# A two-layer diffusion trunk with mixture of experts: the barrier behind the expert loops taken out, layer 1's first adaLN units moved up to them, and the q and k weights issued earlier

## The reference, cut to what matters

```python
for l in range(DEPTH):                       # DEPTH = 2
    mod = split(silu(c) @ ada_w[l] + ada_b[l], 6)          # adaLN shifts, scales, gains
    h = modulate(rmsnorm(x, g[0]), mod[0], mod[1])
    y = mixer(h, ...)                                      # mLSTM, pooling, attention
    x = x + mod[2] * rmsnorm(y, g[1])
    h2 = modulate(rmsnorm(x, g[2]), mod[3], mod[4])
    x = x + mod[5] * rmsnorm(ec_moe(h2, ...), g[3])        # 16 experts, each picks its tokens
    # layer 0 does the same for the context stream
```

## Time and profile before

| | us |
|---|---|
| median of three runs | 2609.04 |
| the three runs | 2605.70, 2609.04, 2611.33 |
| span of the profiled execution | 2604.5 |
| PE busy in it | 2364.8 (91%) |
| DVE, ACT, POOL busy | 694.2, 649.7, 572.9 |

### The profile page before, as it was taken

The page is one execution under the profiler, slowest core; times in us unless marked ns, Lnnn a source line. Parts: engine busy times, 40 slices in busy tenths (PEclk is TensorE's granted clock), DMA queues, the critical chain, the costliest instruction groups (busy, mean ns, idle before and its releaser), DMA issues.

```text
span 2604.5 us, 38764 instructions
## 1 busy us (share of the span) xinstructions
PE 2364.8 (91%) x16132; PEld 1541.6 (59%) x16132; DVE 694.2 (27%) x1403; ACT 649.7 (25%) x1144; POOL 572.9 (22%) x314
## 2 busy tenths in 40 slices
PE   4999999999987699999997699999999689988986
PEld 3778878888876344444443577877887533333332
DVE  3261073101022311111101625054112332222223
ACT  4263253222123110111111435343223301110001
POOL 1143321343510011111111324333465000000000
PEclk8999999999999899999998799999999889999998
DMA  6271440222224699999999336333233579999996
GB/s 241 94 265 64 126 117 14 80 66 86 69 97 160 251 388 390 390 389 392 391 389 354 130 125 248 85 101 86 94 128 110 208 313 402 411 412 410 413 413 251
DMA packets 179894, 596.06 MB, mean 229 GB/s; under 512 B 16040, under 2 KB 57392, under 8 KB 167152
## 3 DMA queue, kind: packets, MB, share of 16 engines
q1 hardware_dynamic: 166448, 563.29, 57.4%
q0 software_dynamic: 10304, 25.99, 3.6%
q10 hardware_dynamic: 3040, 5.31, 0.6%
HBM read 576.63 MB, written 21.07 MB: 229 GB/s over the span
## 4 chain that ended last, share of the span: by engine, by line
PE 69%; DMA 21%; DVE 3%; issue 3%; ACT 2%; POOL 1%; POOLq 0%; SPq 0%; DVEq 0%; ACTq 0%
PE ps L443 19%; PE ps L938 15%; DMA ring_lo<-in_w_gate 11%; PE ps L438 10%; PE ps L858 6%; PE ps L948 6%; DMA zone<-in_w_up 5%; PE ps L879 4%; DMA ring_lo<-in_ada_w 3%; PE ps L754 1%; PE ps L771 1%; PE ps L452 1%; PE ps L957 1%; DMA ring_lo<-in_w_in 1%; PE ps L740 1%
## 5 line engine op out<-in xcount | busy, mean ns | idle before, releaser
L443 PE MATMUL ps<-hi_r,ring_r 128*128 128x512 f32 (+1 forms) x1792 | 474.7, 353 | 3.2 <-POOL ring_r L1870 3.2
L938 PE MATMUL ps<-ring_lo,zone 128*32 128x256 f32 (+1 forms) x3072 | 438.2, 492 | 31.0 <-DMA ring_lo<-in_w_gate 26.8
L443 PEld LDWEIGHTS ps<-hi_r,ring_r 128*128 128x128 f32 x1792 | 316.5, 190 | 50.6 <-POOL ring_r L1870 3.7
L938 PEld LDWEIGHTS ps<-ring_lo,zone 128*32 128x32 f32 (+1 forms) x3072 | 156.5, 124 | 306.4 <-issue 278.9
L1870 POOL TENSOR_TENSOR ring_r<-ring_lo,ring_r 128x2048 fp32r<-128x2048 f32 (+1 forms) x58 | 241.9, 4176 | 367.4 <-ACT ring_r L1031 333.9
L443 PE MATMUL ps<-lo_r,ring_r 128*128 128x512 f32 (+1 forms) x896 | 315.3, 352 | 0.0
L948 PE MATMUL ps<-zone 128*64 128x512 f32 (+1 forms) x2048 | 289.2, 493 | 0.8
L438 PE MATMUL ps<-ring_r,hi_r 128*128 128x512 f32 x736 | 233.2, 398 | 7.1 <-POOL ring_r L1870 6.6
L1981 POOL DMA_INDIRECT zone<-xn_dram,zone x36 | 40.4, 1122 | 843.4 <-DVE zone L1843 769.8
L948 PEld LDWEIGHTS ps<-zone 128*64 128x64 f32 (+1 forms) x2048 | 110.4, 124 | 162.8 <-issue 142.4
L443 PEld LDWEIGHTS ps<-lo_r,ring_r 128*128 128x128 f32 x896 | 169.8, 189 | 23.2
(11 more groups left out here) (303 smaller groups left out, 2771.1 us busy)
## 6 DMA issues: line engine op xcount, KB each, us to landing
ring_lo<-in_w_gate SPq DMA_DIRECT2D x64, 2048.0 KB
zone<-in_w_down SPq DMA_DIRECT2D x64, 2048.0 KB, 22.5
ring_lo<-in_w_up SPq DMA_DIRECT2D x32, 2048.0 KB
zone<-in_w_up SPq DMA_DIRECT2D x32, 2048.0 KB
ring_lo<-in_w_in SPq DMA_DIRECT2D x52, 1024.0 KB
ring_lo<-in_ada_w SPq DMA_DIRECT2D x24, 2048.0 KB
ring_lo<-in_w_branch SPq DMA_DIRECT2D x24, 512.0 KB, 6.2
zone<-v_dram SPq DMA_DIRECT2D x128, 64.0 KB, 1.9
```

Source lines behind the costliest of these rows:

```text
L443: i = mm(dst[:, t0:t0 + tw], b[:, kk, f * P:(f + 1) * P], a[:, k, t0:t0 + tw], start=start and n == 0, stop=stop and n == 2)
L938: i = mm(bank(((2, 4), (3, 5))[s // 2][gi])[j * M:(j + 1) * M, 0:W], xeT[:, k, c0:c0 + M], w[:, k % 4, j * W:(j + 1) * W], start=(k == 0), ...
```

## The change

Five things change.

1. The last `phase_end` of both layers (`ph + 4`) goes on all four engines, and `NPH` becomes 3.
2. adaLN unit 3 goes to slot 3 (in `zone`) in place of slot 0, and SP issues it right behind units 0 to 2.
3. SP issues `("qk", 0)`, the three small loads and `("qk", 1)` of layer 1 ahead of the six loads of `moe_dram`. `("qk", 0)` has slot 1 and waits until PE has used adaLN unit 1; `("qk", 1)` has slot 2 and waits for unit 2.
4. In layer 1 ACT makes the high parts of q and k, ahead of its first square; POOL no longer does.
5. POOL subtracts for the first half at once, and for the second half when five tiles of `x` are there.

```diff
-        ORDER = ((("ada", 0), 0), (("ada", 1), 1), (("ada", 2), 2), (("ada", 3), 0), ...
+        ORDER = ((("ada", 0), 0), (("ada", 1), 1), (("ada", 2), 2), (("ada", 3), 3), ...
...
-        NPH = 4
+        NPH = 3
...
-                phase_end(pe, ph + 4)
...
                 else:
+                    for half in range(2):
+                        _, slot, count, _, _ = units[l, "qk", half]
+                        act.wait_ge(w_ready(slot), 16 * count)
+                        A_(unit_hi(slot, ring_r), unit_lo(slot), ACT.Copy).then_inc(sem("q_hi"), 1)
                     for t in range(NT + 1):
...
-                phase_end(act, ph + 4)
...
-                phase_end(dve, ph + 4)
...
-                if h < 2:
+                if h < 2 and l == 0:
                     pool.wait_ge(w_ready(slot), 16 * units[(l,) + SPLITS[h]][2])
                     G.tensor_copy(unit_hi(slot, ring_r), unit_lo(slot)).then_inc(sem("p_hi"), 1)
-                    pool.wait_ge(sem("p_hi"), 2 * l + h + 1)
+                    pool.wait_ge(sem("p_hi"), h + 1)
+                elif h < 2:
+                    pool.wait_ge(sem("q_hi"), h + 1)
...
+                split(l, 0)
                 if not first:
                     pool.wait_ge(sem("x_tile"), NT - 1)
-                split(l, 0)
...
-                phase_end(pool, ph + 4)
...
-                    return k_[0] > 0 and k_[1] == "ada" and k_[3] < 4
+                    return k_[0] > 0 and (k_[1] == "qk" or k_[1] == "ada" and k_[3] < 4)
...
                 if l + 1 < DEPTH:
-                    for j in range(3):
+                    for j in range(4):
                         load((l + 1, "ada", l + 1, j))
+                    load((l + 1, "qk", 0))
+                    load_vectors(l + 1)
+                    load((l + 1, "qk", 1))
                 if l == 0:
                     sp.wait_ge(sem("y_added"), 16 * len(SETS[l]) * NE)
                     for t in range(nt(l)):
                         sp.dma_start(xn[:, t, :], moe_dram[l][t * P:(t + 1) * P, :]).then_inc(sem(f"moe_in{t}"), 16)
                 if l + 1 < DEPTH:
-                    load((l + 1, "ada", l + 1, 3))
                     sp.wait_ge(sem("x_tile"), l * PER["x_tile"] + NT)
```

More of the change, by code:

```diff
@@ L302, in kn512 @@
             return w[:, c:c + 512].rearrange("(k p) n -> p k n", p=P)
-        ORDER = ((("ada", 0), 0), (("ada", 1), 1), (("ada", 2), 2), (("ada", 3), 0), (("qk", 0), 1), (("qk", 1), 2), (("v", 0), 0),
+        ORDER = ((("ada", 0), 0), (("ada", 1), 1), (("ada", 2), 2), (("ada", 3), 3), (("qk", 0), 1), (("qk", 1), 2), (("v", 0), 0),
                  (("v", 1), 1), (("ada", 4), 2), (("ada", 5), 0), (("ada", 6), 1), (("ada", 7), 2), (("ada", 8), 0), (("o", 0), 1),
@@ L2050, in load_branch, with load_vectors @@
                     sp.dma_start(branch_w(q, False).rearrange("p (k n) -> p k n", k=KB), src).then_inc(sem(f"mg_in{q % 2}"), 16)
-                def load_vectors():
+                def load_vectors(l):
                     sp.wait_ge(sem("pads_set"), 1)
@@ L2072, in _ @@
                     if key[1:] == ("qk", 0):
-                        load_vectors()
+                        load_vectors(l)
                     if key[1:] == ("vn", 0):
```

## The result

The changed kernel takes 2612.05 us, median of 20 runs (2606.79 to 2615.54); the kernel before 2607.86, median of 20 (2604.49 to 2611.33). The ratio is 1.0016, 95% interval 1.001 to 1.0022: slower by 4.2 us. The forecast was 2.5 less than before, 2606.5, with a range of 2601 to 2612; the sign is wrong, and the time is just outside the range.

What follows compares the result with a forecast made beforehand. PE, busy 91% of the span, was taken as the bound, so only its idle time at two places could move: +0.4 at the layer boundary and −2.9 at layer 1's end gave −2.5 us, 2606.5, range 2601 to 2612.

Steps and rivals of the forecast that it cites:

- The barrier after layer 0: Between layers 0 and 1: without it ACT could begin 1.1 us earlier, and PE's adaLN units move up to 1412.1.
- The loads put ahead of the sums: At the layer boundary: the experts' sums are issued 4.4 us later, and ACT's first square begins 6.4 later, at 1433.0.
- the rival of the late sums: At the boundary: ACT begins at 1437.7, 4.7 us more, so the whole is +2.2, 2611.2, no change; chance 0.12.
- what it called wrong: Sign at the boundary: prediction wrong if ACT's first square is before 1430 or after 1438, or no DVE instruction is stretched.
- The wait of ACT for unit 3 goes: In layer 1's chain of tiles: ACT no longer waits for adaLN unit 3 before `ada_rows`, a gain of 5.0 us.
- POOL's second subtraction: Behind the fifth tile of x: it holds DVE's last tile for 4.6 us, bounds 0 and 5.1.
- the rule on two SBUF inputs: At DVE's L1403 and L1405: two-SBUF-input instructions and GpSimd instructions reading SBUF exclude each other, costing 4.6 us.
- POOL's wait goes: At layer 1's first q and k product: POOL's first subtraction ends before 1435, PE no longer waits, gain 5.6 us.
- The barrier at the end of layer 1: At the end of layer 1: ACT starts beside DVE's additions, so the last stretch starts 2.9 us earlier, bounds 0 and 3.0.

Runs made afterwards that it cites:

- e1: The changed kernel with one lone drain of POOL behind layer 0's expert loop, on which no engine waits: 2606.99 us, ratio 0.9995 to the kernel before.
- e4: The kernel before with only the last barriers of both layers taken out: 2605.81 us, ratio 0.9998.
- e7: The changed kernel with a drain of POOL in every turn of layer 0's expert loop: 2608.06 us, ratio 1.0006 to the kernel before.
- e2: The changed kernel with the three small loads issued behind the experts' sums: 2607.47 us, ratio 1.0002 to the kernel before.
- e5: The changed kernel with the edits of e1, e2 and e3 together: 2600.83 us, ratio 0.9976 to the kernel before.
- e6: The changed kernel with e1's drain, sums issued before q, k and small loads, ACT's copies behind `ada_rows`, both POOL subtractions behind the sixth tile: 2601.15 us, ratio 0.9981.
- e3: The changed kernel with POOL's second subtraction waiting for the sixth tile of x, not the fifth: 2607.34 us, ratio 1.0002 to the kernel before.
- e8: The kernel before with only the barrier at the end of layer 1 taken out: 2602.85 us, ratio 0.9989.

## Why the prediction was wrong, by its own steps

*"The barrier after layer 0": this step failed.* It priced the barrier by who waits at that place, 1.1 us for ACT, and took the 4.06 of the drain to vanish with it. e1, e4 and e7 show that the work of a drain is kept and done by POOL's next one. There the kernel waits for it. That the drain cost little where it stood is right: without the barrier e4's first square comes 1.0 earlier. What the prediction didn't ask is what comes due later on POOL if the drain is gone. In the changed kernel that is 4.0 (5.80 for 1.78, and PE's wait 9.79 for 5.78); the stretch has 4.4, and e1 gives back 4.5, both with its scatter. The term stood at nothing in the sum, and in every rival.

*"The loads put ahead of the sums": the mechanism right, the size 5.0 short; this term failed too.* The prediction had the first square 6.4 later, from a down product that ends at 1412.1; against that end it came 11.4 later (25.95 less 14.56). Of the 5.0, 0.9 is the issue of `("qk", 0)`, at +5.0 for +4.1, since PE used unit 1 later; 3.3 is SP, which took 13.3 from there to `("qk", 1)`, not the 10.0 of the earlier trace rows, nor the 11.3 of the earlier trace rows; 0.9 is the landing of the second half, 5.9 for 5.0.

It is the rival of the late sums, which had 0.12: 20.9 and its 4.7 make +25.6, and +25.95 is 0.3 past it. The profile's own 1436.9 looks to be inside the bounds (1431.7 to 1437.7) only because this execution ended its down product 1.1 earlier; on the prediction's scale it is 1438.0, at the very edge of what it called wrong.

The 10.0 had been read as the price of three small issues. The traces fit another reading, which no run tests by itself: it is the time until the load ahead of them has landed. In the kernel before, `("qk", 0)` landed at 1464.7 and SP came free of the small loads at 1464.2; in the changed one that load took 13.5 us to land,

```profile
DMA to landing us min/median/max: 13.5/13.5/13.5
```

that is until 1429.4, and SP came free at 1429.2. In e2, e5 and e6 too SP is free of the three 0.2 to 0.4 before the last big load ahead has landed. And the queue itself ran late: by PE's matmuls unit 2 was there at +9.7 and unit 3 at +15.6 (+6.9 and +12.3 forecast). What held the queue up is not shown.

*"The wait of ACT for unit 3 goes": right.* PE has used unit 3 by 1428.5, and no wait of ACT before `ada_rows` is left.

*"POOL's second subtraction": right, 4.2 for 4.6.* The held instruction is L1432 (4.91 less 0.75), a TENSOR_SCALAR that reads SBUF, for which the prediction had no row; e3 moves the hold behind the last tile and PE starts 3.8 earlier. The forecast leaned on the wrong rule for it. It named the rule on two SBUF inputs and looked for the hold at L1403 and L1405; the hold came on the TENSOR_SCALAR ahead of them, and whether the subtraction would have held those two no row here shows. The Trainium skill ("SBUF — State Buffer", section "Who interferes with whom") has a second rule that bears on it: copies and TENSOR_SCALAR can run in a mode that uses both port pairs, and then they exclude GpSimd too. This case's rows agree: TENSOR_SCALAR 4.91 for 0.75, and in e6 a copy of 16 columns 4.26 for 0.17. In e6 a TENSOR_TENSOR with an input in PSUM (L1386) ran its 0.18 inside POOL's second subtraction, as the PSUM form did in the earlier trace rows.

*"POOL's wait goes": right.* POOL's first subtraction ended at 1436.0 (before 1435 forecast), long before it was needed, and DVE released the product. From the issue of `x_dram` (1463.07) to DVE's first low part it was 7.6 (7.7 forecast), and 5.07 more to PE (5.0 forecast).

*"The barrier at the end of layer 1": right*, 3.06 for 2.9, and e8 measures it alone as 0.9989.

*The sum.* By its parts: +4.7 at the boundary (+0.4 forecast), +4.0 for the drain (no term), −3.1 at the end (−2.9): +5.6. The timed difference is +4.2 with 2.6 to 5.7 as its interval (the ratio's bounds by 2607.9). The profiled pair differs by 7.2; the −1.1 and +2.2 of the other two stretches are in it, which no term explains.

Two errors of one sign made the miss. With the drain's term alone the sum would have been +1.5, with the late boundary alone +1.8: both within the range. The mended e5 has the short drain again and 5.5 us of the boundary back, and comes out faster than the kernel before; the 3.1 us at the end of layer 1 are the one gain over that kernel which stands clear in the profiles.

## What to carry to other kernels

Before a barrier is taken out, look for what its drains did besides waiting: on POOL, with many transfers issued before it, the drain has a length that the next one inherits, so keep a drain where the engine is idle anyway and drop only the waiting. Price the issue of small DMAs behind a big one by when the big one will have landed, not by the time they took elsewhere, and look at merged rows of issues one by one, since a wait can lie between them. A wide elementwise instruction of POOL should start when DVE has nothing left on the path, and two in a row are worse than one.

## What the runs showed of the hardware

- A drain of POOL behind transfers that had landed took 0.29 us with 3 indirect ones since the one before, 0.38 with 4 (e7), 1.53 with 18 (layer 1's loop, in the kernel before), 4.06 with 49: 0.08 to 0.1 us for each. At the merge the part behind the last TENSOR_TENSOR was 0.5 us with five plain transfers and 4.5 with these and the 49 left over (5.80 less 1.3), the same for each.
- It doesn't get cheaper with time: the 4.0 us were there 588 us after the last scatter as they were 7 us after it (1415.8 to 1422.5, in the kernel before).
- A drain right behind the write of `xn_dram` took 28.7 us; the write landed 28.6 us after its issue.
- The issue of a small load of one shape (128x8x16) on SP took from 0.4 us (e2) to 7.8 (e5). The three together took 9.4 us in the kernel before and 12.2 in the changed one, and ended 0.5 and 0.2 before the big load ahead had landed.
- A DVE copy of 128x16 took 4.26 us beside a subtraction of POOL, and 0.17 without (e6 and the changed kernel).
